# One decoder layer with a 64-expert MoE: expert loop, overflow loop and closing stage in one block

## What is computed

```python
def moe_ffn(h, lw):
    x = h.reshape(-1, h.shape[-1])
    idx, wts = route(x, lw['router_w'], lw['router_bias'])          # 8 of 64 experts for each token
    routed = routed_experts(x, idx, wts, lw['expert_w_gate'], lw['expert_w_up'], lw['expert_w_down'])
    shared = (jax.nn.silu(x @ lw['shared_w_gate']) * (x @ lw['shared_w_up'])) @ lw['shared_w_down']
    return routed + shared

    f = moe_ffn(h2, lw)
    x = x + g2 * rmsnorm(f, lw['post_ffn_g'])
```

## Time and profile before

| | |
|---|---|
| median of three runs | 2027.73 us |
| profiled execution, time | 2029.44 us |
| profiled execution, span (first to last instruction) | 2027.7 us |
| TensorE busy | 87% of the span |
| VectorE (DVE) busy | 57% |
| ScalarE (ACT) busy | 44% |
| GpSimd (POOL) busy | 33% |
| mean granted TensorE clock | 0.942 of full speed |
| moved by DMA | 458.31 MB, 226 GB/s |

### The profile page before, as it was taken

One profiled execution on the slowest core, in us unless ns is written; L12 is line 12 of the kernel. 1 busy time (PEld: TensorE's weight loads), 2 busy tenths in 40 slices (PEclk: granted clock), 3 DMA queues, 4 the chain that ended last, 5 costly groups with the idle time before them and its releaser, 6 DMA issues. The chain is left out here.

```text
span 2027.7 us, 24495 instructions
## 1 busy us (share of the span) xinstructions
PE 1767.8 (87%) x7667; PEld 1201.4 (59%) x7668; DVE 1148.6 (57%) x1512; ACT 889.7 (44%) x1320; POOL 659.8 (33%) x550
## 2 busy tenths in 40 slices
PE   6968999967898898685999999999999999996554
PEld 1214444533335666545888888888888888884221
DVE  0124565645123556464777777777777777773323
ACT  0001111104234545313676766667676666763211
POOL 0003565650000000012455555555555555551000
PEclk9979999987999899887999999999999999998777
DMA  9934556557776211574798989999999999986422
GB/s 281 361 121 137 176 160 181 161 159 253 234 227 208 73 61 50 199 286 168 226 312 296 309 300 293 313 297 316 300 298 310 301 313 311 292 261 185 158 83 73
DMA packets 146350, 458.31 MB, mean 226 GB/s; under 512 B 29079, under 2 KB 38145, under 8 KB 120332
## 3 DMA queue, kind: packets, MB, share of 16 engines
q1 hardware_dynamic: 114147, 383.03, 52.5%
q0 software_dynamic: 30720, 69.83, 15.2%
q10 hardware_dynamic: 1364, 3.99, 0.5%
HBM read 404.43 MB, written 86.56 MB: 242 GB/s over the span
## 5 line engine op out<-in xcount | busy, mean ns | idle before, releaser
L2097 PE MATMUL ps<-hi_gu,xT_hi 128*128 128x512 f32 x768 | 309.1, 402 | 0.0
L2143 DVE TENSOR_TENSOR lo_gu<-raw_gu,hi_gu 128x1024 fp32r<-128x1024 f32 x256 | 304.2, 1220 | 4.5
L2097 PE MATMUL ps<-hi_gu,xT_lo 128*128 128x512 f32 x768 | 300.6, 391 | 0.0
L2097 PE MATMUL ps<-lo_gu,xT_hi 128*128 128x512 f32 x768 | 298.9, 389 | 0.0
L2035 ACT ACTIVATE hi_gu<-raw_gu 128x1024 fp32r<-128x1024 f32 x256 | 260.8, 1064 | 0.0
L481 POOL TENSOR_TENSOR prod<-kring,qbc 128x512 f32<-128x512 f32 x128 | 165.3, 1327 | 279.6 <-DMA kring<-in_cache_k 234.5
L565 PE MATMUL ps<-w_in_sb,hT 128*128 128x512 f32 (+1 forms) x576 | 251.6, 598 | 0.3 <-ACT hT L500 0.3
L1998 POOL DMA_INDIRECT acc_d<-yb,tokb x96 | 227.9, 2374 | 43.5 <-ACT yb L2049 28.3
L1979 POOL DMA_INDIRECT xg<-h_d,tokb x96 | 101.7, 1059 | 367.9 <-PE ps L2083 366.6
L565 PEld LDWEIGHTS ps<-w_in_sb,hT 128*128 128x128 f32 (+1 forms) x576 | 102.6, 179 | 142.6 <-issue 142.2
L2049 ACT ACTIVATE yb<-ps,wslot 128x1024 f32<-128x1024 f32 x96 | 107.0, 1115 | 137.4 <-PE ps L2114 137.4
(11 more groups left out here) (323 smaller groups left out, 2676.9 us busy)
## 6 DMA issues: line engine op xcount, KB each, us to landing
raw_gu<-in_expert_w_gate SPq DMA_DIRECT2D x64, 1024.0 KB, 7.9
raw_gu<-in_expert_w_up SPq DMA_DIRECT2D x64, 1024.0 KB, 11.7
raw_dn<-in_expert_w_down SPq DMA_DIRECT2D x64, 1024.0 KB, 8.1
kring<-in_cache_k SPq DMA_DIRECT2D x128, 256.0 KB, 2.8
vring<-in_cache_v SPq DMA_DIRECT2D x128, 256.0 KB, 3.0
adaw<-in_ada_w SPq DMA_DIRECT2D x12, 2048.0 KB, 11.0
a<-acc_d SPq DMA_DIRECT2D x16, 512.0 KB, 5.7
acc_d<-zeros SPq DMA_DIRECT2D x14, 512.0 KB
```

The costliest lines, as they stand in the source:

```text
L2097: last = pe.matmul(ps[:, 2 + b % 2, :].rearrange("p (a f) -> p a f", a=2), x[b % 2][:, k, :], w[:, :, k * F:(k + 1) * F], start=(k == 0 an ...
L2143: dve.tensor_tensor(lo_cut(n, u), raw_cut(n, u), hi_cut(n, u).bitcast(F32), ALU.subtract).then_inc(lo_made, 1)
```

## The change

The three blocks become one. What each engine did in each of them becomes a function, and each engine runs its functions one behind the other, without a barrier between. What the barriers ordered is now ordered by waits on named semaphores:

- POOL enters its overflow loop's body only after the last `down` (`dn_mm`), ACT's first step in that body waits for `hb_made`, and PE's for `y_here`. With no block used, only POOL's wait is executed.
- SP, before its first load of sums, waits for all scatters (`rows_out`, in addition to POOL's own wait) and for `o_ended`.
- PE, before `gate_up(3)`, waits until ACT has emptied the last PSUM result of the expert loop (`y_here`).

`hx2` gets six buffers instead of two, three of them where the expert loop had its turned rows, and a semaphore each. SP issues all six `load_hidden` ahead of its wait for the scatters, and none inside the loop over tiles.

```diff
+        def overflow_pool(pool):
+            pool.sem_inc(o_x_tr, 1)
+            pool.wait_ge(dn_mm, MAIN)
+            with blocks_over(pool) as o:
...
-        hx2 = [place(f"hx2_{j}", 53 + 4 * j, [P, KC, P]) for j in range(2)]
+        hx2 = [place(f"hx2_{j}", 53 + 4 * j if j < 3 else 177 + 4 * j, [P, KC, P]) for j in range(T9 - NWIN)]
...
-                def load_hidden(t):
-                    u = t - NWIN
-                    if u >= 2:
-                        sp.wait_ge(gu6, u - 1)
-                    sp.dma_start(hx2[u % 2][:, :, :], h2T_d[t].rearrange("p (k t) -> p k t", k=KC)).then_inc(hx2_in[u % 2], 16)
+            def load_hidden(t):
+                u = t - NWIN
+                sp.dma_start(hx2[u][:, :, :], h2T_d[t].rearrange("p (k t) -> p k t", k=KC)).then_inc(hx2_in[u], 16)
...
-                load_hidden(NWIN)
-                load_hidden(NWIN + 1)
-                load_sums(0)
+            for t in SH:
+                load_hidden(t)
+            for j in range(2):
+                sp.wait_ge(rows_out[j], 16 * (MAIN // 2))
+            sp.wait_ge(o_ended, 1)
+            load_sums(0)
...
-                    if t in SH and t + 2 < T9:
-                        load_hidden(t + 2)
                     store(t)
...
+            pe.wait_ge(y_here, MAIN)
             pe.wait_ge(sw2_in, 48)
             gate_up(NWIN)
...
+        with nc.Block() as block:
+            @block.sync
+            def _(sp):
+                experts_sp(sp)
+                overflow_sp(sp)
+                finish_sp(sp)
```

More of the change, by code:

```diff
@@ new lines, in experts_sp @@
+        def experts_sp(sp):
+            for n in range(EARLY, NE):
+                if n >= RAWS:
+                    sp.wait_ge(gu_mm, last_block(n - RAWS) + 1)
+                e = load_gate_up(sp, n)
+                if n >= RAWS:
+                    sp.wait_ge(dn_mm, last_block(n - RAWS) + 1)
+                load_down(sp, n, e)
+            sp.wait_ge(dn_mm, last_block(NE - 3) + 1)
+            for h, w in enumerate((sw_gate, sw_up)):
+                sp.dma_start(s_gu2[:, h, :], w[0].rearrange("(p k) f -> p (k f)", k=KC)).then_inc(sw2_in, 16)
+            sp.dma_start(s_dn2[:, :, :], sw_down[0].rearrange("(p c) n -> p c n", c=FC)).then_inc(sw2_in, 16)
+            for t in range(T9):
+                if t == 0:
+                    sp.wait_ge(dn_mm, last_block(NE - 2) + 1)
+                if t == 6:
+                    sp.wait_ge(dn_mm, MAIN)
+                at_row, rows = rows_at(t)
+                sp.dma_start(x1_5[t][0:rows, :], x1_d[at_row:at_row + rows, :]).then_inc(x1_in, 16)
@@ new lines, in experts_pe, with turn_x, gate_up, down @@
+        def experts_pe(pe):
+            def turn_x(b):
+                pe.wait_ge(xg_in[b % 2], 16 * (b // 2) + 16)
+                if b:
+                    pe.wait_ge(xT_made, b)
+                for k in range(KC):
+                    last = pe.transpose(ps[:, k // 4, (k % 4) * P:(k % 4 + 1) * P],
+                                        xg[b % 2].rearrange("t (p k) -> t k p", k=KC)[:, k, :], ident)
+                last.then_inc(x_tr, 1)
+            def gate_up(b):
+                n = expert_of(b)
+                pe.wait_ge(xT_made, b + 1)
+                if b >= 2:
+                    pe.wait_ge(hT_made, b - 1)
+                wh, wl = hi_gu[n % 2], lo_gu[n % RAWS]
+                for k in range(KC):
+                    if b == first_block(n) and k % 2 == 0:
+                        pe.wait_ge(lo_made, CUTS * n + k // 2 + 1)
+                    for x, w in ((xT_hi, wh), (xT_hi, wl), (xT_lo, wh)):
+                        last = pe.matmul(ps[:, 2 + b % 2, :].rearrange("p (a f) -> p a f", a=2), x[b % 2][:, k, :],
+                                         w[:, :, k * F:(k + 1) * F], start=(k == 0 and x is xT_hi and w is wh),
+                                         stop=(k == KC - 1 and x is xT_lo))
+                last.then_inc(gu_mm, 1)
+            def down(b):
+                n = expert_of(b)
+                pe.wait_ge(hT_made, b + 1)
+                if b == first_block(n):
+                    pe.wait_ge(lo_made, CUTS * n + CUTS)
+                if b >= 2:
+                    pe.wait_ge(y_here, b - 1)
+                wh, wl = hi_dn[n % 2], lo_dn[n % RAWS]
+                for half in range(2):
+                    cols = slice(512 * half, 512 * half + 512)
+                    for ch in range(FC):
+                        for h, w in ((hT_hi, wh), (hT_hi, wl), (hT_lo, wh)):
+                            last = pe.matmul(ps[:, 4 + 2 * (b % 2) + half, :], h[b % 2][:, ch, :], w[:, ch, cols],
+                                             start=(ch == 0 and h is hT_hi and w is wh), stop=(ch == FC - 1 and h is hT_lo))
+                last.then_inc(dn_mm, 1)
+            def turn_h(b):
+                pe.wait_ge(hb_made, b + 1)
+                for ch in range(FC):
+                    last = pe.transpose(ps[:, 2 + b % 2, ch * P:(ch + 1) * P],
+                                        hb[b % 2].rearrange("t (p c) -> t c p", c=FC)[:, ch, :], ident)
+                last.then_inc(h_tr, 1)
+            turn_x(0)
+            for b in range(MAIN):
+                if b + 1 < MAIN:
+                    turn_x(b + 1)
+                gate_up(b)
+                if b:
+                    down(b - 1)
+                turn_h(b)
+            down(MAIN - 1)
@@ new lines, in finish_act, with gated, turned, norm @@
+        def finish_act(act):
+            def gated(t):
+                u = t - NWIN
+                act.wait_ge(gu6, u + 1)
+                if u >= 2:
+                    act.wait_ge(h6_made, u - 1)
+                act.activation(sg6[u % 2][:, :], ps[:, u % 2, 0:F], ACT.Sigmoid).then_inc(sg6_here, 1)
+            def turned(t):
+                u = t - NWIN
+                act.wait_ge(h6_tr, u + 1)
+                if u >= 2:
+                    act.wait_ge(dn6, u - 1)
+                act.activation(hT6[u % 2].rearrange("p c t -> p (c t)"), ps[:, u % 2, 0:F], ACT.Copy).then_inc(hT6_here, 1)
+            def norm(t):
+                _, rows = rows_at(t)
+                act.wait_ge(summed, t + 1)
+                if t:
+                    act.wait_ge(ss6, t)
+                if t >= 2:
+                    act.wait_ge(scaled, t - 1)
+                act.activation(junk6[0:rows, :], a0[t % A0][0:rows, :], ACT.Square, accum_out=s6[t % 2][0:rows, 0:1]
+                               ).then_inc(ss6, 1)
+                act.wait_ge(ss6, t + 1)
+                act.activation(s6[t % 2][0:rows, 1:2], s6[t % 2][0:rows, 0:1], ACT.Sqrt, bias=c("eps", rows), scale=1.0 / D
+                               ).then_inc(rt6, 1)
+            for t in range(T9):
+                if t + 1 in SH:
+                    gated(t + 1)
+                if t in SH:
+                    turned(t)
+                norm(t)
@@ new lines, in finish_pe, with gate_up, turn_down @@
+        def finish_pe(pe):
+            def gate_up(t):
+                u = t - NWIN
+                pe.wait_ge(hx2_in[u], 16)
+                if u >= 2:
+                    pe.wait_ge(hT6_here, u - 1)
+                for k in range(KC):
+                    last = pe.matmul(ps[:, u % 2, :].rearrange("p (a f) -> p a f", a=2), hx2[u][:, k, :],
+                                     s_gu2[:, :, k * F:(k + 1) * F], start=(k == 0), stop=(k == KC - 1))
+                last.then_inc(gu6, 1)
+            def turn_down(t):
+                u = t - NWIN
+                pe.wait_ge(h6_made, u + 1)
+                for ch in range(FC):
+                    last = pe.transpose(ps[:, u % 2, ch * P:(ch + 1) * P],
+                                        h6[u % 2].rearrange("t (p c) -> t c p", c=FC)[:, ch, :], ident)
+                last.then_inc(h6_tr, 1)
+                pe.wait_ge(hT6_here, u + 1)
+                if u >= 2:
+                    pe.wait_ge(summed, t - 1)
+                for half in range(2):
+                    for ch in range(FC):
+                        last = pe.matmul(ps[:, 4 + 2 * (u % 2) + half, :], hT6[u % 2][:, ch, :],
+                                         s_dn2[:, ch, 512 * half:512 * half + 512], start=(ch == 0), stop=(ch == FC - 1))
+                last.then_inc(dn6, 1)
+            pe.wait_ge(y_here, MAIN)
+            pe.wait_ge(sw2_in, 48)
+            gate_up(NWIN)
+            for t in SH:
+                if t + 1 < T9:
+                    gate_up(t + 1)
+                turn_down(t)
@@ L2387, in _ @@
-                for t in range(T9):
-                    if t + 1 in SH:
-                        gated(t + 1)
-                    if t in SH:
-                        turned(t)
-                    norm(t)
+                experts_act(act)
+                overflow_act(act)
+                finish_act(act)
             @block.tensor
             def _(pe):
-                def gate_up(t):
-                    u = t - NWIN
-                    pe.wait_ge(hx2_in[u % 2], 16 * (u // 2) + 16)
-                    if u >= 2:
```

(5 more changed lines are left out.)

674 lines of the change are left out of this document (278 added, 396 removed).

## The result

The median went from 2027.05 us (four runs) to 1966.10 us (four runs, 1962.14 to 1970.14), 61.0 less; the prediction was 1964. The ratio is 0.9696, 95% interval 0.9671 to 0.9721: faster by 3.0%. The profiled execution took 1970.14, with a span of 1968.4.

The account below looks back on a forecast made before the run. PE bounds the expert loop; in the closing stage it waits 73.1 us for rows. Opening -9.1, four steps -(104.1 - 46.5), clock restart +2.7 sum to -64.0: 1964 us against the median, 8-in-10 range 1957 to 1977.

Parts of the forecast that it names:

- The steps: Closing stage, downs of tiles 3 to 7: each step 3.4 + 6.9 + 1.3 = 11.6 us; four take 46.5 instead of 104.1.
- ACT's cover: Closing-stage steps: ACT is free 9.1 after the down, its sigmoid due after 10.3 at the earliest, leaving 1.2 us.
- The opening: Start of tile 3's down: 1891.3 instead of 1900.37, a gain of 9.1 us.
- the arithmetic of the queue: Ahead of tile 1's sums: 6.68 MB at 0.395 MB per us, 16.9 us from 1860, so 1876.9.
- the latency of the first sums: Opening: sums of tile 1 land later than the queue's arithmetic gives; 3 us taken, between ends of 0 and 5.2.
- The restart of the clock: Tile 3's down: PE idles some 5 us before it and runs at a lower clock; 2.7 us added, ends 0 and 2.9.
- The tail: From the down of tile 7 to the end of the span: stays at 23.2 us.
- The clock did not fall in every step: Rival, closing-stage steps: the clock falls in each 1 us wait for ACT, three more steps pay 2.7; 1972 us, 12%.
- the scatter have to wait until the row tiles were through: Rival, opening: six row tiles hold back the last scatter, tile 3's down 5.4 us later; 1969 us, 13%.
- No other wait of 26 appeared: Rival, closing stage: another wait replaces the rows, steps stay at 26 and only the opening gains; about 2019 us, 2%.
- the expert loop is as long as it was: Rival, expert loop: the joined program's longer code slows it; 0.67 us more per block eats the whole gain; 5%.
- the drain, the barriers and the overflow loop as hidden by the queue of row tiles: Opening: these cost nothing any more because the queue covers them; with a shorter queue they would show.

Follow-up runs that it names:

- e1: Kernel before, three blocks kept, with six row tiles resident and issued ahead of the first sums: 1974.18 us, ratio 0.9747.
- e3: Changed kernel with only two row tiles ahead of the first sums, the other four issued behind the sums of tile 2: 1953.99 us, ratio 0.9652.
- e5: Changed kernel with the first barrier put back, between expert loop and overflow loop: 1972.05 us, ratio 0.9746.
- e6: Changed kernel with the second barrier put back, between overflow loop and closing stage: 1974.15 us, ratio 0.9756.
- e2: Changed kernel (joined program) with two row buffers and the loads of tiles 5 to 8 inside the loop as before: 2012.84 us, ratio 0.9925.
- e4: Changed kernel with ACT and DVE taking tile 3 and the first half of tile 4 ahead of the first sums: 1965.67 us, ratio 0.9704.
- e8: Changed kernel, rows of tiles 3 and 4 before residual rows, other rows behind first sums, ACT and DVE working further ahead: 1946.21 us, ratio 0.9615.
- e9: e8 with the rows of tile 5 also issued ahead of the first sums: 1943.74 us, ratio 0.9598.

## Why the prediction was right

**The steps.** Predicted 11.6, measured 11.3; the down of one tile to the next gate and up to the next down, as written. The 1.3 ran from the weight load of the first turn, which begins 0.6 before gate and up has ended (1925.02 against 1915.83 + 9.79), so on top of a full gate and up it was too much; from the end of gate and up to the next down it is 0.73 (1911.19 - 1903.58 - 6.88). ACT's cover held: in steps 2 to 4 nothing but PE's own work and its short wait for the turned copy is in the chain, and ACT waits up to 1.5 for PE before its sigmoid, where the prediction had 1.2 of cover. e1 shows that the rows alone do this.

**The opening.** Down of tile 3: predicted 1891.3, which is 32.3 after the last scatter, measured 34.0. The gain of this term was 7.3, not 9.1. The term that was too small is what comes on top of the arithmetic of the queue, called the latency of the first sums: between ends of 0 and 5.2 I took 3. The arithmetic gave 17.9 after the scatter, DVE had the sums of tile 1 after 22.4, so it was 4.6, close to what the trace before had shown. Not all of it is latency. The sum has the queue move 0.79 MB in 2 us throughout, but it moved 0.59 from 1868 to 1870, 0.54 from 1870 to 1872 and 0.45 from 1880 to 1882: 0.79 MB less in all, so I estimate that some 2 us of the 4.6 are a slower queue. The chain behind it took 11.6 instead of 11.3. PE started 2 later than predicted (11.1 against 9), which nobody waited for.

**The restart of the clock.** Predicted 2.7; the down of tile 3 took 5.95 instead of 3.70, 2.25, with a mean granted clock of 0.62 from 1897.6 to 1903.6, in part at 1.2 and in part at 2.4 GHz. e3, in which PE waits 0.80 there instead of 5.39, has 3.70 and a clock of 1.00. The size of this term can't be foretold any better from these runs: behind the same wait of 5.39 that down took 6.58 in e1, 5.49 in e5 and 5.20 in e6.

**The tail.** Predicted 23.2, measured 1968.4 - 1945.14 = 23.3.

**The sum** came out at 63.9 against 64.0 because two errors cancel: the opening gained 1.8 less, four steps with the restart took 47.5 instead of 49.2. The agreement to 0.1 is luck; the terms are known to one or two us. The mechanism was right: e1 and e2 show the two halves, 51.0 and 13.3.

**The rivals.** The clock did not fall in every step: it is 1.00 from 1910 to 1950, in spite of a wait of 0.52 for ACT in each. Nor did the scatter have to wait until the row tiles were through. While SP's queue was full, from 1866 to 1868, q0 had next to nothing, as in the earlier trace rows:

```profile
q1 hardware_dynamic: 191, 0.70, 99.6%
...
q0 software_dynamic: 5, 0.00, 0.1%
```

but from 1870 to 1872 it had the larger share:

```profile
q0 software_dynamic: 71, 0.29, 72.6%
q1 hardware_dynamic: 71, 0.25, 34.6%
```

and the sums were issued 9.9 after the last scatter, against 9.6 when POOL's wait ended before. The Trainium skill ("DMA: Bandwidth & Descriptors", section "Queues, rings and completion order") says that a DMA engine takes turns between the queues it has work for, a packet at a time. The trace agrees once the scatter's data moves, with 71 packets of either queue from 1870 to 1872; but that data begins only some 5 after the issue. In the kernel before, a scatter issued at 1845.59, with q1 at 5.9% from 1847 to 1848, had data moving by 1848, which suggests that a full SP queue delays the start; one scatter doesn't show it. No other wait of 26 appeared, and the expert loop is as long as it was.

**What the text had not seen.** It took the drain, the barriers and the overflow loop as hidden by the queue of row tiles, and wrote that with a shorter queue they would show. That reason was wrong. e2 and e3 have the shorter queue, and nothing shows: SP issues the first sums 9.6 and 9.5 after the last scatter, before POOL's drain has begun, and the down of tile 3 comes at 28.7 and 28.5. These costs are gone because SP no longer waits for POOL's drain; e5 and e6 have the long queue, and either barrier brings them back. And e3 shows that the queue itself, in the order the change gave it, took another 8 from the gain.

## What to carry to other kernels

When a wait for a transfer repeats in every step, look at what the issue of the transfer stands behind in its queue's own list; if memory allows, take it out of the loop, but put it behind whatever the first consumer needs soonest. A barrier costs what its slowest member does last, here POOL's wait for the last scatter and a drain behind it, so taking away one of two barriers in a row may give almost nothing. And a wait that is taken off one engine's path often stands again one item later in a list written by hand (e4): keep the lead on all engines of the chain from tile to tile, as in e8. There it came together with the early rows; no run here has the lead alone.

## What was not expected of the hardware

The drain behind POOL's indirect DMAs is nearly constant, 5572 ns before, 5575 after and 5572 in e5, although the wait for their landing has ended ahead of it. And the price of a pause on PE is not. Behind the same wait of 4.22 the last down of the stage took 5.40 in the kernel before, 5.10 in e3, 6.36 in e4 and 6.75 in e6, with granted clocks of 0.72 in e3 and 0.55 in e6. Even whether the clock falls isn't settled by the length of the wait; the last down of e8, at a granted clock of 1.00:

```profile
1924.11 3.70 PE L2407 MATMUL ps<-s_dn,hT 128*128 128x512 f32 x8 [2.17 <-ACT hT L2359]
```

and that of e9, at 0.68:

```profile
1923.11 5.40 PE L2408 MATMUL ps<-s_dn,hT 128*128 128x512 f32 x8 [2.16 <-ACT hT L2360]
```
